# A decoder trunk on one core: output-weight splits moved in the last head, four staging buffers for the down projection, layer two's operand split chunk by chunk

## The reference, cut to what matters

```
x = x + conformer_conv(rmsnorm(x, g), ...)                  # layer 0, 1024 tokens x 1024 features
x = x + swiglu(rmsnorm(x, g), w1[0], w3[0], w2[0])          # D_FF = 2816
k, v = rmsnorm(x, kv_norm_g) @ w_k, ... @ w_v               # 8 heads
x = x + diff_attention(rmsnorm(x, g), k, v, w_q, ...)       # layer 1; ends in rmsnorm(o) @ w_o
x = x + swiglu(rmsnorm(x, g), w1[1], w3[1], w2[1])
return rmsnorm(x, final_norm_g)                             # all float32
```

## Time and profile before

| | us |
|---|---|
| median of 3 runs (2367.91 to 2370.8) | 2368.04 |
| the profiled execution's own time | 2371.16 |
| its span, first to last instruction | 2369.4 |
| mean granted PE clock in it | 0.992 |

### The profile page before, as it was taken

The page is one execution under the profiler, slowest core; times in us unless marked ns, Lnnn a source line. Parts: engine busy times, 40 slices in busy tenths (PEclk is TensorE's granted clock), DMA queues, the critical chain, the costliest instruction groups (busy, mean ns, idle before and its releaser), DMA issues.

```text
span 2369.4 us, 28710 instructions
## 1 busy us (share of the span) xinstructions
PE 2302.7 (97%) x11205; PEld 1884.7 (80%) x11205; DVE 1609.1 (68%) x2473; ACT 904.2 (38%) x1569; POOL 67.4 (3%) x51
## 2 busy tenths in 40 slices
PE   7999989999999999999999999989999999999998
PEld 6884868888788888887777777778788888878998
DVE  6996589999466634445677767764868777763455
ACT  5321532222344422223455555652632323232344
POOL 0000000000000000002111111000000000000000
PEclk9999989999999999999999999999999999999999
DMA  4110223333233333332111111211122232244575
GB/s 139 45 36 18 80 72 95 93 92 97 83 102 91 103 91 98 98 94 63 32 37 36 36 36 44 86 32 45 54 62 86 83 90 76 85 161 146 160 229 185
DMA packets 280324, 200.88 MB, mean 85 GB/s; under 512 B 7973, under 2 KB 258686, under 8 KB 280190
## 3 DMA queue, kind: packets, MB, share of 16 engines
q1 hardware_dynamic: 280190, 199.04, 27.7%
HBM read 180.14 MB, written 18.87 MB: 84 GB/s over the span
## 4 chain that ended last, share of the span: by engine, by line
PE 84%; DVE 8%; DMA 3%; ACT 3%; issue 1%; SPq 0%; DVEq 0%; ACTq 0%
PE ps L1979 26%; PE ps L1981 25%; PE ps L1980 25%; PE ps L2127 3%; PE ps L1962 3%; DMA raw<-in_ffn_w_dram 3%; DVE cacc L1414 2%; DVE cvA L1414 2%; PE ps L2082 1%; DVE Wl L1942 1%; DVE sc L1657 1%; ACT sc L1108 1%; ACT Wh L1319 1%; PE ps L2044 1%; DVE Wl L1339 0%
## 5 line engine op out<-in xcount | busy, mean ns | idle before, releaser
L1979 PE MATMUL ps<-Sh,Wl 128*128 128x512 f32 x1616 | 657.5, 407 | 20.1 <-DVE Sl L1497 6.8
L1981 PE MATMUL ps<-Sh,Wh 128*128 128x512 f32 x1616 | 633.3, 392 | 0.0
L1980 PE MATMUL ps<-Sl,Wh 128*128 128x512 f32 x1616 | 632.3, 391 | 0.0
L1979 PEld LDWEIGHTS ps<-Sh,Wl 128*128 128x128 f32 x1616 | 305.4, 189 | 98.6 <-issue 28.2
L1981 PEld LDWEIGHTS ps<-Sh,Wh 128*128 128x128 f32 x1616 | 304.8, 189 | 66.0
L1980 PEld LDWEIGHTS ps<-Sl,Wh 128*128 128x128 f32 x1616 | 305.9, 189 | 60.4 <-issue 3.8
L1339 DVE TENSOR_TENSOR Wl<-raw,Wh 128x1024 fp32r<-128x1024 f32 (+1 forms) x178 | 213.3, 1199 | 92.4 <-ACT Wh L898 91.0
L898 ACT ACTIVATE Wh<-raw 128x1024 fp32r<-128x1024 f32 (+1 forms) x178 | 183.2, 1032 | 155.4 <-DMA raw<-in_ffn_w_dram 127.7
L1979 PE MATMUL ps<-Dh,Wl 128*128 128x256 f32 (+1 forms) x528 | 170.7, 323 | 9.2 <-DVE Wl L1942 4.8
L1942 DVE TENSOR_TENSOR Wl<-raw,Wh 128x1024 fp32r<-128x1024 f32 x66 | 80.8, 1224 | 131.3 <-ACT Wh L1319 131.2
L1980 PE MATMUL ps<-Dl,Wh 128*128 128x256 f32 (+1 forms) x528 | 169.0, 320 | 0.0
(11 more groups left out here) (251 smaller groups left out, 3899.5 us busy)
## 6 DMA issues: line engine op xcount, KB each, us to landing
raw<-in_ffn_w_dram SPq DMA_DIRECT2D x214, 512.0 KB, 3.9
raw<-in_pw_w_dram SPq DMA_DIRECT2D x32, 512.0 KB, 4.0
raw<-in_ffn_w_dram SPq DMA_DIRECT2D x32, 448.0 KB, 3.8
g_dram<-st SPq DMA_DIRECT2D x36, 256.0 KB, 2.0
graw<-g_dram SPq DMA_DIRECT2D x22, 256.0 KB, 3.8
graw<-g_dram SPq DMA_DIRECT2D x44, 128.0 KB, 3.7
xrow<-in_x_dram SPq DMA_DIRECT2D x8, 512.0 KB, 6.3
raw<-in_w_q_dram SPq DMA_DIRECT2D x8, 512.0 KB, 4.7
```

Source lines behind the costliest of these rows:

```text
L1979: pe.matmul(dst, ll, rh, start=start, stop=False)
L1980: pe.matmul(dst, lh, rl, start=False, stop=False)
L1981: return pe.matmul(dst, lh, rh, start=False, stop=stop)
```

## The change

```
-WO_AT = {(LAST - 1, 6): 0, (LAST - 1, 7): 1, (LAST, 1): 2, (LAST, 2): 3}
+WO_AT = {(LAST - 1, 6): 0, (LAST - 1, 7): 1, (LAST, 0): 2, (LAST, 1): 3}
+def wo_split_in(t):            # the blocks whose splits belong to row t
+    h, i = t // TB, t % TB
+    blocks = [WO_AT[h, i]] if (h, i) in WO_AT else []
+    if h == LAST:
+        blocks += [RESULTS[j][0] + 4 for j in results_in(i) if RESULTS[j][1]]
+    return blocks
 # SP, attention loads: block 2 ahead of read_back(1)
+                if h == LAST:
+                    load(WO0 + 2, cols(wo_heads, 2))
                 if h >= LAST - 1:
                     read_back(h - LAST + 1)
-            for n in range(2, KC):
+            for n in range(3, KC):
 # ACT row (and out_norm in DVE's row likewise from 2 to 3)
-                if i == (1 if last else 2) and h:
+                if i == 2 and h:
                     out_root(h - 1, 4 if last else 0, TB)
 # DVE row: wo_lo taken from the end of the row to here
                 if i < TB - 1:
                     score_rows(t + 1, 0)
                     score_rows(t + 1, 1)
+                for n in wo_split_in(t - 1):
+                    wo_lo(n)
...
 # out_last in DVE and PE: n by n, both halves
-                hf, n = j // KC - 2, j % KC
+                n, hf = (j - 2 * KC) // 2, j % 2
 # ACT, layer two's operand (then the squares as before)
-                    act.wait_ge(wo_ev, 4 * KC)
+                    act.wait_ge(wo_ev, 2 * KC + 2 * n + hf + 1)
 # PE
-            ffn(F1, OP_F1, lambda r: (wo_ev, 4 * KC), beside_f1)
+            ffn(F1, OP_F1, lambda r: (wo_ev, 2 * KC if r < 2 else 4 * KC), beside_f1)
 # DVE, after the last results
+                if j >= 2 * KC - 3 and j % 2:          # behind results 13 and 15
+                    lo(F1.block0 + (j - 2 * KC + 3) // 2)
-            for j in range(2 * KC, 4 * KC):
-                add_out(j)
-                if j == 2 * KC + 1:
-                    lo(F1.block0)
-                    lo(F1.block0 + 1)
-            for n in range(KC):
+            for n in range(KC + 1):
                 for hf in F1.halves:
-                    operand_low(OP_F1 * KC + 2 * n + hf, hf, n, ...)
+                    if n < KC:
+                        add_out(2 * KC + 2 * n + hf)
+                for hf in F1.halves:
+                    if n:
+                        operand_low(OP_F1 * KC + 2 * n - 2 + hf, hf, n - 1, ...)
 # down projection: draw = raw + two tiles of 4 KB at G_AT + 32 KB, used as draw[d % 4] by SP, ACT, DVE
             def down_load(d):
-                if d >= 2:
-                    sp.wait_ge(dw_lo, d - 1)
+                if d >= 4:
+                    sp.wait_ge(dw_lo, d - 3)
+                elif d >= 2:
+                    sp.wait_ge(up_mm, ALL_PRODUCTS)
 # SP: loads 2 and 3 before the last hidden store
+                            if u == UNITS - 1 and j == 3:
+                                down_load(2)
+                                down_load(3)
                             unit_store(u, j)
-                sp.dma_start(grow[:, :], ...)           # the final gain: was here, before step 2's load
-                for d in range(2, STEPS_D):
+                for d in range(4, STEPS_D):
                     down_load(d)
-                    if d >= 4:
-                        hidden_load(d)
+                    hidden_load(d)
+                    if d == 8:
+                        ...                             # the four g_out waits and the load of grow
 # DVE: down_low(d) makes Wl and Dl of step d; EARLY = 2 of them inside the last up unit
                 if more:
                     up_low(u + 1, S3)
                     up_low(u + 1, S4)
+                else:
+                    for d in range(EARLY):
+                        down_low(d)
                 result_of(u, 3, A22, E_21, q6, LA)
```

More of the change, by code:

```diff
@@ L127 @@
 STEPS_D = len(PARTS) * FC
+EARLY = 2
 def ubank(q):
@@ L417, in trunk @@
         raw = [at(f"raw{r}", [P, KC, P], F32, RAW_AT + r * 4 * KB) for r in range(2)]
+        draw = raw + [at(f"draw{r}", [P, KC, P], F32, G_AT + (32 + 4 * r) * KB) for r in range(2)]
         Wh = [at(f"Wh{r}", [P, KC, P], F32R, W_AT + r * 8 * KB) for r in range(RING)]
@@ L561, in trunk @@
         g_st = [sem(f"g_st{hf}") for hf in range(2)]
-        dw_in = [sem(f"dw_in{r}") for r in range(2)]
+        dw_in = [sem(f"dw_in{r}") for r in range(4)]
         dg_in = [sem(f"dg_in{r}") for r in range(4)]
@@ L695, in down_load @@
             def down_load(d):
-                if d >= 2:
-                    sp.wait_ge(dw_lo, d - 1)
+                if d >= 4:
+                    sp.wait_ge(dw_lo, d - 3)
+                elif d >= 2:
+                    sp.wait_ge(up_mm, ALL_PRODUCTS)
                 else:
                     sp.wait_ge(u_lo, ALL_PRODUCTS)
-                sp.dma_start(raw[d % 2][:, :, :], down[d % FC]).then_inc(dw_in[d % 2], 16)
+                sp.dma_start(draw[d % 4][:, :, :], down[d % FC]).then_inc(dw_in[d % 4], 16)
             def hidden_load(d):
@@ L739, in second_layer @@
                                 hidden_load(2 * j + 1)
-                for j in range(4):
-                    sp.wait_ge(g_out[j], 16 * (UNITS // 2))
-                sp.dma_start(grow[:, :], a["final_norm_g"].unsqueeze(0).broadcast_to([P, D])).then_inc(grow_in, 16)
-                for d in range(2, STEPS_D):
+                for d in range(4, STEPS_D):
                     down_load(d)
-                    if d >= 4:
-                        hidden_load(d)
+                    hidden_load(d)
+                    if d == 8:
+                        for j in range(4):
+                            sp.wait_ge(g_out[j], 16 * (UNITS // 2))
+                        sp.dma_start(grow[:, :], a["final_norm_g"].unsqueeze(0).broadcast_to([P, D])) \
+                            .then_inc(grow_in, 16)
                     t = y_behind(d - 8)
@@ L1313, in _ @@
             for d in range(STEPS_D):
-                act.wait_ge(dw_in[d % 2], 16 * (d // 2 + 1))
+                act.wait_ge(dw_in[d % 4], 16 * (d // 4 + 1))
                 if d < RING:
@@ L1318, in _ @@
                     step_done(act, d - RING)
-                act.activation(flat(Wh[down_slot(d)]), flat(raw[d % 2]), ACT.Copy).then_inc(dw_hi, 1)
+                act.activation(flat(Wh[down_slot(d)]), flat(draw[d % 4]), ACT.Copy).then_inc(dw_hi, 1)
                 w = PARTS[d // FC][1]
@@ L1692, in add_out @@
             def add_out(j):
-                n, hf = RESULTS[j] if j < 2 * KC else (j % KC, j // KC - 2)
+                n, hf = RESULTS[j] if j < 2 * KC else ((j - 2 * KC) // 2, j % 2)
                 dve.wait_ge(wo_mm, j + 1)
@@ L1721, in row @@
                     att_lo(h + 2, Q_R)
-                if i == (2 if last else 3) and h:
+                if i == 3 and h:
                     out_norm(h - 1, 4 if last else 0, TB, h if last else h - 1)
@@ L1738, in row @@
                     operand_low_part(k, hf)
[L1739 to L1745, removed]
+                if i == TB - 1 and not last:
                     qk_low(h + 1, 1)
@@ L1767, in _ @@
                     row(h, i)
+            for n in wo_split_in(HEADS * TB - 1):
+                wo_lo(n)
             out_norm(LAST, 4, TB, LAST + 2)
@@ L1776, in _ @@
                     wo_lo(RESULTS[j][0] + 4)
+                if j >= 2 * KC - 3 and j % 2:
+                    lo(F1.block0 + (j - 2 * KC + 3) // 2)
             if not operand_done:
                 operand_low_part(LAST, LB)
-            for j in range(2 * KC, 4 * KC):
-                add_out(j)
-                if j == 2 * KC + 1:
-                    lo(F1.block0)
-                    lo(F1.block0 + 1)
-            for n in range(KC):
-                for hf in F1.halves:
-                    operand_low(OP_F1 * KC + 2 * n + hf, hf, n, col("ffn_norm_g", KC + n))
+            for n in range(KC + 1):
+                for hf in F1.halves:
+                    if n < KC:
+                        add_out(2 * KC + 2 * n + hf)
+                for hf in F1.halves:
+                    if n:
+                        operand_low(OP_F1 * KC + 2 * n - 2 + hf, hf, n - 1, col("ffn_norm_g", KC + n - 1))
             lo(F1.block0 + 2)
@@ L1889, in result_of, with down_low @@
                     dve.tensor_tensor(st[:, i, :], to, st[:, i, :], ALU.mult).then_inc(u_g, 1)
+            def down_low(d):
+                dve.wait_ge(dw_hi, d + 1)
+                dve.tensor_tensor(flat(Wl[down_slot(d)]), flat(draw[d % 4]), flat(Wh[down_slot(d)]).bitcast(F32),
+                                  ALU.subtract).then_inc(dw_lo, 1)
+                w = PARTS[d // FC][1]
+                dve.wait_ge(dg_hi, d + 1)
+                dve.tensor_tensor(Dl[d % 4][:, 0:w], graw[d % 4][:, 0:w], Dh[d % 4][:, 0:w].bitcast(F32),
+                                  ALU.subtract).then_inc(dg_lo, 1)
             ffn(F1, beside_f1)
@@ L1940, in _ @@
             for d in range(STEPS_D):
[L1941 to L1947, removed]
```

(2 more changed lines are left out.)

## The result

| | before | after |
|---|---|---|
| median, us | 2368.98 (4 runs, 2367.91 to 2370.8) | 2344.61 (4 runs, 2344.1 to 2345.37) |
| the profiled execution's own time | 2371.16 | 2344.1 |
| its span | 2369.4 | 2342.3 |
| mean granted PE clock in it | 0.992 | 0.996 |

The ratio is 0.9893 [0.9882, 0.9905], 24.4 us less. Forecast were 2345.0 and 2337 to 2355: right. The page's first part has the same numbers of instructions as before and PE busy for 9 us less; the other 18 us were idle time.

What follows compares the result with a forecast made beforehand. PE, busy 97% of the span, bounds the kernel, so gains come from its idle or half-speed places. 12.0 - 0.6 + 5.3 + 7.2 = 23.9, less 0.9: 2368.04 - 23.0 = 2345.0 us, range 2337 to 2355.

Steps and rivals of the forecast that it cites:

- The five terms: Last head: PE idle places of 1.1, 0.5, 4.66, 0.6 and 2.06 us go; with 3.9 of clock 12.8, counted 12.0.
- the 4.66: Last head, PE's wait for output block 2: earlier load and split, and bank 6 free sooner, gain all 4.66 us.
- `out_root` in row 2: Last head, ACT: takes 3.0 us, over before PE's next transposes; by the skill's price the gain falls by up to 1.6.
- Second feed-forward: Its start: DVE alternates additions and operand parts, one long wait becomes eight short ones, 0.6 us lost.
- that rival: Second feed-forward: short waits drop the clock, 5 us lost, time 2350, chance 0.10.
- Down projection's start: Earlier low parts gain 3.0 us, full speed in step 0 gains 2.3, together 5.3, bounds 3 and 6.
- 256-wide steps: Down projection: four buffers bring steps to 2.88 us, 3.67 with a row turn, 7.2 gained, bounds 0 and 7.5.
- rival three: 256-wide steps: four transfers in flight are as slow as two, nothing gained there, time 2352, chance 0.08.
- the slower rival: 256-wide steps: loads in flight slow each other until four take longer than two did, time 2373, chance 0.03.
- the late low parts: Last head: low parts behind the scores make transposed weights late, gain only 5 us, time 2352, chance 0.12.
- does not do what it says: Block 2 still late, last head gains 3 us, down start keeps half speed, time 2356, chance 0.05.
- The allowance of 0.9: Whole kernel: 0.9 us taken off the summed gain, since half-speed stretches likely differ between executions.

Runs made afterwards that it cites:

- root_row1: The changed kernel with `out_root` and `out_norm` of the last head back in rows 1 and 2: 2347.78 us, 0.9901 beside the kernel before.
- lo_end: The changed kernel with DVE's low parts of the output blocks back at the end of their rows: 2351.29 us, 0.9915 beside the kernel before.
- down_only: The kernel before with only the down projection's edits (four buffers, load order, early low parts): 2358.13 us, 0.9944.
- chunk_only: The kernel before with only layer two's operand made chunk by chunk, DVE alternating additions and operand parts: 2371.07 us, 0.9999.
- head_only: The kernel before with only the last head's edits (split turns, load order, `out_root`, low parts behind scores): 2356.97 us, 0.9941.
- early0: The changed kernel with the down projection's first low parts again after the last up result, four buffers kept: 2349.51 us, 0.9905 beside the kernel before.

## Why the prediction was right, point by point

- **What bounds it.** PE's idle places and the clock behind them were the matter: each engine ran as many instructions as before, and 25.8 us went.
- **Last head, 12.0 forecast, 13.2 measured.** The five terms and the clock summed to 12.8; all came, and the 0.8 taken off for low parts that would be late did not. The steps behind the 4.66 were right: block 2 and the bank were both in it, as root_row1 shows; lo_end, with both still moved, has no 4.66. Block 2's low part was put at 1544.4 and came at 1540.33. What I had not seen is that the new turns would have made new idle places without the place behind the scores (1.7 us in lo_end).
- **`out_root` in row 2** hid, at one load and its activation to 0.01 us. ACT's timeline of the kernel after:

```profile
1550.80 1.28 ACT L1172 ACT_TABLE_LOAD   x1
1552.09 0.30 ACT L1172 ACTIVATE stats<-stats,small 128x4 f32<-128x4 f32 x1
...
1555.50 0.60 ACT L1142 ACTIVATE ATh<-ps 128x512 fp32r<-128x512 f32 x1 [1.60 <-PE ps L1990]
```

  ACT then waits 1.60 for PE. The Trainium skill ("ScalarE: Activation LUTs", "What ACT_TABLE_LOAD costs") adds a drain of 1380 ns to a switch; two would have been 2.8 us, by estimate. No gap of this kind is in the trace, behind a load (0.01 us) or ahead of one (0.02), and nothing was lost.
- **Second feed-forward, -0.6 forecast, -0.26 measured.** The mechanism was exact: the first matmul stood 15.30 behind addition 15 (forecast 15.3), and short waits took the place of the long ones. They are listed at 0.70 to 0.92, since a matmul's listed end lies behind the start of the next; by starts a chunk took 2.52 against 1.36 without a wait, so 1.16 each (forecast 1.2). There are four, as in the prediction's sum, not the eight of its text, and before there were two, not one. The term left out is the first block, 0.50 shorter: before, the second token half's operand came late too, and the first two matmuls took 0.91 instead of 0.46. The short waits cost no clock (1.00 over 1642 to 1652): that rival fell.
- **Down projection's start, 5.3 forecast, 5.70 measured.** Idle time 1.46, 2.97 gained (3.0). Step 0 took 5.56, which gave 2.73 where I took 2.3 of 2.85, because I could not tell whether 1.5 us would drop the clock. It did not in any of the seven traces with 1.46 to 1.60. That this term fits owes something to luck: against the 7.1 of three other executions at that place it would have been 1.5.
- **256-wide steps, 7.2 forecast, 7.09 measured.** 36 steps of 2.88 and 6 with a row turn of 3.67, as counted; the 0.4 missing is in the step behind each turn, 2.95 six times. ACT's square and root, put at about 3.5, took 2.7 and hid. The transfers were no bound: rival three and the slower rival fell, as did the late low parts and "does not do what it says".
- **The allowance of 0.9** for half speed that differs between executions was the right kind of term and is not to be settled in size: the kernel before moves by 8 us, and by job the gain is 24.4 or 27.0. The traces' 25.8 lies between, 1.9 above the 23.9 of the sum, and the gain by the medians, 24.4, is 1.4 above the 23.0 forecast. That the time came within 0.4 of the forecast is in part luck: the median that it started from, 2368.04, had three runs; with the fourth it is 2368.98, and that 0.9 hid most of the 1.4.

## What to carry to other kernels

An engine that works in order makes every consumer wait for whatever stands ahead: put a producer's work behind the piece that is wanted next, and look, at each long wait, for the second thing that is nearly as late. The number of staging buffers followed here from one division, the round of load, split and release over the consumer's step. Splitting a barrier by chunks gives nothing if the engine that feeds both sides then alternates; let it first finish what holds up the pipe.

## What was not expected of the hardware

- **Half speed behind an idle place of 2 to 2.5 us comes in some executions and not in others.** Behind the 2.06 the clock was 0.66 over 5 us in the kernel before, in lo_end and in down_only, 1.00 in chunk_only. Behind the 2.42 it was 1.00 in the kernel before, 0.71 in head_only and 0.73 in down_only. Longer places dropped it in every trace that has them, the 4.66 (before, chunk_only, down_only) and the 4.44 (before, head_only, chunk_only, early0), but for stretches of different length: behind the 4.44 it was 0.66 over 10 us before and 0.83 in the other three. The 2.38 in root_row1 had 0.80 behind it. Places of 1.46 to 1.71 never dropped it. Same code, same work before each; what decides between them is open.
- **Loads landed later when the steps took them faster.** Issues of the weight blocks in the 256-wide steps (count, KB each, median us from issue to landing), kernel before, then after:

```profile
raw<-in_ffn_w_dram SPq DMA_DIRECT2D x39, 512.0 KB, 3.8
```

```profile
raw<-in_ffn_w_dram SPq DMA_DIRECT2D x19, 512.0 KB, 4.3
draw<-in_ffn_w_dram SPq DMA_DIRECT2D x18, 512.0 KB, 4.9
```

  While the loads ran, the rate was 220 GB/s at 0.69 of the DMA engines' time before (2230 to 2340) and 245 at 0.74 after (2210 to 2310); the 211 of the stretch to 2333, shown above, has some 15 us almost without loads at its end. With three buffers the medians were 4.8 and 4.9, so it is not the fourth load in flight that does it. The Trainium skill ("DMA: Bandwidth & Descriptors", "Latency and other measured facts") would allow, by estimate, up to 1.8 us more by latency at high load; 0.5 to 1.1 came, and nothing here tells latency from sharing of the DMA engines.
- **Code that no edit touched starts up to 2.8 us apart.** The first mark of the ledger, ahead of all edits, lay at 1514.39 after and 1515.69 before; over all profiled executions it goes from 1513.51 (down_only) to 1516.34 (down_first). What makes that is open. Gains of 1 or 2 us are to be read between near marks in one trace, not from its end.
